# Third block's tables in a four-layer decoder trunk: VectorE makes six of eight chunks one step later, GpSimd makes the other two

## The reference, cut to what matters

```python
h = rms_norm(x, norm_mix[i]); x = x + mixer(h)
h = rms_norm(x, norm_ffn[i]); x = x + (swiglu if i % 2 == 0 else moe_swiglu)(h)
# the S5 mixer of layer 1 (64 groups of 16 channels, 64 complex states each)
mag, ang = exp(lam_re * dt), lam_im * dt;  a = mag * (cos(ang) + 1j * sin(ang))
x_t = a * x_(t-1) + B u_t;   y_t = Re(C x_t) + d * u_t;   out = GLU(gelu(y))
```

## Time and profile before

| | before |
|---|---|
| median of 3 runs | 1737.85 us |
| the profiled execution | 1736.63 us, its span 1735.1 us |
| busy, share of the span: PE, weight loads of PE | 96%, 89% |
| DVE, ACT, POOL | 75%, 58%, 12% |
| chain that ended last: PE, DVE, ACT | 75%, 10%, 6% |

### The profile page before, as it was taken

How to read it: one execution, slowest core, us unless ns; L and a number is a source line. 1 busy time by engine, 2 the same in 40 slices (tenths; PEclk the granted TensorE clock), 3 DMA queues, 4 the chain that set the end, 5 groups by cost and what they waited for, 6 DMA issues and landing times.

```text
span 1735.1 us, 26693 instructions
## 1 busy us (share of the span) xinstructions
PE 1662.9 (96%) x10979; PEld 1542.7 (89%) x10979; DVE 1295.1 (75%) x1283; ACT 1002.0 (58%) x920; POOL 214.6 (12%) x230
## 2 busy tenths in 40 slices
PE   6998999989999999999989999999999999999996
PEld 6998899878899999999879999998998999999995
DVE  5478998785688888888867555446548888888886
ACT  5554333243677777777645353335556777777773
POOL 4406991010000000000310000000000000000001
PEclk9999999989999999999999999999999999999998
DMA  7336987575489999999943254454344999999993
GB/s 305 126 119 205 309 279 263 201 277 185 146 333 365 347 373 354 380 353 357 375 145 110 75 216 182 147 192 149 120 146 183 363 352 353 375 346 368 357 382 144
DMA packets 53482, 449.28 MB, mean 259 GB/s; under 512 B 6736, under 2 KB 8944, under 8 KB 16640
## 3 DMA queue, kind: packets, MB, share of 16 engines
q1 hardware_dynamic: 48480, 430.40, 66.0%
q0 software_dynamic: 4896, 17.35, 2.8%
HBM read 426.63 MB, written 21.10 MB: 258 GB/s over the span
## 4 chain that ended last, share of the span: by engine, by line
PE 75%; DVE 10%; ACT 6%; issue 4%; DMA 3%; POOL 1%; POOLq 0%; DVEq 0%; ACTq 0%; SPq 0%
PE PS L323 22%; PE PS L325 22%; PE PS L324 22%; DVE wlo L375 3%; ACT whi L368 3%; DMA yg<-expert_rows,offi 1%; DMA expert_rows<-ysb 1%; PE PS L2119 1%; PE PS L1757 1%; PE PS L2082 1%; PE PS L2083 1%; ACT h L503 1%; PE PS L1325 1%; PE PS L916 1%; PE PS L496 1%
## 5 line engine op out<-in xcount | busy, mean ns | idle before, releaser
L375 DVE TENSOR_TENSOR wlo<-raw,whi 128x3072 fp32r<-128x3072 f32 (+1 forms) x278 | 856.3, 3082 | 181.8 <-ACT whi L368 181.0
L368 ACT ACTIVATE whi<-raw 128x3072 fp32r<-128x3072 f32 (+1 forms) x278 | 705.8, 2540 | 326.5 <-PE PS L325 310.1
L323 PE MATMUL PS<-wlo,hT_hi 128*128 128x384 f32 (+3 forms) x1840 | 594.7, 323 | 1.9 <-DVE wlo L375 1.4
L324 PE MATMUL PS<-whi,hT_lo 128*128 128x384 f32 (+3 forms) x1840 | 591.6, 322 | 0.0
L325 PE MATMUL PS<-whi,hT_hi 128*128 128x384 f32 (+3 forms) x1840 | 591.4, 321 | 0.0
L323 PEld LDWEIGHTS PS<-wlo,hT_hi 128*128 128x128 f32 x1840 | 347.7, 189 | 6.0 <-DVE wlo L375 1.7
L324 PEld LDWEIGHTS PS<-whi,hT_lo 128*128 128x128 f32 x1840 | 347.7, 189 | 2.9
L325 PEld LDWEIGHTS PS<-whi,hT_hi 128*128 128x128 f32 x1840 | 347.5, 189 | 0.3
L323 PE MATMUL PS<-wlo,mhi 128*128 128x512 f32 x352 | 143.5, 408 | 0.0
L324 PE MATMUL PS<-whi,mlo 128*128 128x512 f32 x352 | 139.1, 395 | 0.0
L325 PE MATMUL PS<-whi,mhi 128*128 128x512 f32 x352 | 139.0, 395 | 0.0
(11 more groups left out here) (392 smaller groups left out, 2073.0 us busy)
## 6 DMA issues: line engine op xcount, KB each, us to landing
raw<-in_weights SPq DMA_DIRECT2D x203, 1536.0 KB, 8.0
raw<-in_weights SPq DMA_DIRECT2D x73, 1024.0 KB, 7.1
raw<-s_tables SPq DMA_DIRECT2D x8, 1536.0 KB, 7.1
expert_rows<-ysb POOLq DMA_DIRECT2D x14, 512.0 KB, 9.7
s_tables<-g_out SPq DMA_DIRECT2D x8, 640.0 KB, 4.3
t_af<-s_rows_af SPq DMA_DIRECT2D x32, 128.0 KB, 4.0
s_tables<-g_out SPq DMA_DIRECT2D x8, 512.0 KB, 4.6
raw<-in_weights SPq DMA_DIRECT2D x3, 1152.0 KB, 9.5
```

The lines of the kernel that those rows point to most:

```text
L323: pe.matmul(o, sh, mlw, start=start, stop=False, skip_group_check=True)
L324: pe.matmul(o, sl, mh, start=False, stop=False, skip_group_check=True)
L368: act.activation(whi[p0 % SPL][:, 0:n], raw[p0 % RAW][:, 0:n], ACT.Copy).then_inc(hi_done, 1)
L375: dve.tensor_tensor(wlo[p0 % SPL][:, 0:n], raw[p0 % RAW][:, 0:n], whi[p0 % SPL][:, 0:n].bitcast(F32), ALU.subtract).then_inc(lo_done, 1)
```

## The change

Four things change. `s5_turns_dve` parts 0 to 6 move to earlier places in the attention, and only part 7 is left ahead of `proj_dve`. DVE makes the powers and taps of chunks 0 to 5 only, one dense step later than before (powers of chunk j - 1 in step j, taps of chunk j - 2 at its start), so none in step 0 and none after the last step. POOL makes those of chunks 6 and 7 in a new function, after its own eight chunks and ahead of `decay`, with loads and stores of its own queue; ACT, DVE and SP wait for these stores instead. And the four matmuls of the row of scales go behind the first `k_block`, in both attentions.

```diff
@@ sp_program
-                for c in range(KC):
-                    if p0 == base["dense0"] + ND["g", c] + SPL + RAW:
+                for c in range(DVE_TABLES):
+                    if p0 == base["dense0"] + ND["g", c + 1] + SPL + RAW:
...
-            s5_taps_store(sp, KC - 1)
@@ sb_pe
-            for b in range(3):
-                k_block(b)
+            k_block(0)
+            row_of_rs(pe, norm)
+            k_block(1)
+            k_block(2)
@@ sb_dve (a == 0): after k_out(5) parts 0 and 1, after low(4) part 2, after q_out(7) part 3,
@@ after k_out(6) part 4, after out_low(5) part 5, after softplus(7) part 6, after out_low(7) part 7
-                for part in range(4, 8):
-                    s5_turns_dve(dve, part)
+                s5_turns_dve(dve, 7)
@@ dense_dve
+        DVE_TABLES = KC - 2
-                if f == 0 and j == 0:
-                    s5_powers_dve(dve, 0)
                 if f == 0 and j >= 2:
-                    s5_taps_dve(dve, j - 1)
+                    s5_taps_dve(dve, j - 2)
...
-                if f == 0:
-                    (s5_powers_dve if j else s5_taps_dve)(dve, j)
+                if f == 0 and 1 <= j <= DVE_TABLES:
+                    s5_powers_dve(dve, j - 1)
...
-            if f == 0:
-                s5_taps_dve(dve, JD - 1)
@@ s5_tables_pool
             for b in range(2):
                 pool.wait_ge(s5_tw[b], 16 * (KC // 2))
+            s5_last_tables_pool(pool)
+        def s5_last_tables_pool(pool):
...
+            for n, c in enumerate(range(DVE_TABLES, KC)):
+                written = 16 * (KC // 2) + 32 * n
+                pool.dma_start(ff["t_bs"][:, 0, :], s5_bc[c, :, 256:512]).then_inc(s5_bs[0], 16)
+                pool.dma_start(ff["t_bs"][:, 1, :], s5_bc[c, :, 0:256]).then_inc(s5_bs[0], 16)
+                for r in range(4):
...
+                    pool.dma_start(af[32 * r:32 * r + 32].rearrange("p n q s -> p (n q s)"),
+                                   src.to_broadcast([32, 8 * P])).then_inc(s5_bs[0], 16)
+                pool.wait_ge(s5_bs[0], 16 * (KC // 2) + 96 * (n + 1))
...
+                pool.tensor_copy(o_g[:, :, :, 0, :], cn_)
+                pool.tensor_tensor(o_g[:, :, 0, 1:5, :], cr, pr, ALU.mult)
...
+                pool.dma_start(tabs[c, :, T_G], flat[:, T_G]).then_inc(s5_tw[0], 16)
+                pool.wait_ge(s5_tw[0], written + 16)
...
+                pool.tensor_tensor(o_w[:, :, 0], af[:, :, 0], b0, ALU.mult)
...
+                pool.dma_start(tabs[c, :, T_W], flat[:, 0:1024]).then_inc(s5_tw[0], 16)
+            pool.wait_ge(s5_tw[0], written + 32)
@@ s5_act, s5_dve (and s5_loads for c >= DVE_TABLES)
-            act.wait_ge(s5_gw, 16 * KC)
-            act.wait_ge(s5_ww, 16 * KC)
+            act.wait_ge(s5_gw, 16 * DVE_TABLES)
+            act.wait_ge(s5_ww, 16 * DVE_TABLES)
+            act.wait_ge(s5_tw[0], 16 * (KC // 2) + 32 * (KC - DVE_TABLES))
```

More of the change, by code:

```diff
@@ L257, in hybrid_trunk @@
                    ("ta_c", [P, ST, 8], F32), ("ta_s", [P, ST, 8], F32),
-                   ("tb_c", [P, ST, 8], F32), ("tb_s", [P, ST, 8], F32), ("t_pow", [P, ST, 2, 4], F32))
+                   ("tb_c", [P, ST, 8], F32), ("tb_s", [P, ST, 8], F32), ("t_pow", [P, ST, 2, 4], F32),
+                   ("t_af2", [P, 4, 2, P], F32))
         setup = stage(("pad_setup", [P, 42 * KB], F32),
@@ L415, in sp_program @@
                     s5_taps_load(sp, 0)
-                for c in range(KC):
-                    if p0 == base["dense0"] + ND["g", c] + SPL + RAW:
+                for c in range(DVE_TABLES):
+                    if p0 == base["dense0"] + ND["g", c + 1] + SPL + RAW:
                         s5_powers_store(sp, c)
-                        if c + 1 < KC:
+                        if c + 1 < DVE_TABLES:
                             s5_powers_load(sp, c + 1)
-                    if p0 == base["dense0"] + ND["u", c] + SPL + RAW:
+                    if p0 == base["dense0"] + ND["u", c + 1] + SPL + RAW:
                         s5_taps_store(sp, c)
-                        s5_taps_load(sp, c + 1)
-            s5_taps_store(sp, KC - 1)
+                        if c + 1 < DVE_TABLES:
+                            s5_taps_load(sp, c + 1)
             s5_loads(sp)
@@ L813, in first_columns, with row_of_rs @@
             last.then_inc(w_used, 1)
+        def row_of_rs(pe, norm):
             if norm == 0:
@@ L1210, in sb_dve @@
             k_out(5)
+            if a == 0:
+                s5_turns_dve(dve, 0)
+                s5_turns_dve(dve, 1)
             softplus(3)
@@ L1218, in sb_dve @@
             low(4)
+            if a == 0:
+                s5_turns_dve(dve, 2)
             out_low(3)
@@ L1222, in sb_dve @@
             if a == 0:
-                s5_turns_dve(dve, 0)
+                s5_turns_dve(dve, 3)
             softplus(5)
@@ L1229, in sb_dve @@
             if a == 0:
-                s5_turns_dve(dve, 1)
+                s5_turns_dve(dve, 4)
             split_lo(dve, b0 + 9)
@@ L1236, in sb_dve @@
             if a == 0:
-                s5_turns_dve(dve, 2)
+                s5_turns_dve(dve, 5)
             softplus(6)
@@ L1242, in sb_dve @@
             if a == 0:
-                s5_turns_dve(dve, 3)
+                s5_turns_dve(dve, 6)
             low(7)
@@ L1674, in s5_tables_pool @@
                 s5_decay_pool(pool, c).then_inc(s5_dec, 1)
+        def s5_last_tables_pool(pool):
+            flat = ff["t_out"][:].rearrange("p a n -> p (a n)")
+            o_g = flat[:, T_G].rearrange("p (r q i o) -> p r q i o", r=4, q=2, i=5)
+            o_w = flat[:, 0:1024].rearrange("p (n q s) -> p n q s", n=4, q=2)
+            cn_ = ff["t_bs"][:, 0, :].rearrange("p (r q o) -> p r q o", r=4, q=2)
+            bt = ff["t_bs"][:, 1, :].rearrange("p (q a s) -> p q a s", q=2, a=1)
+            pa, af = ff["t_pow"], ff["t_af2"]
+            tp = ff["t_tmp"][:].rearrange("p (r i o) -> p r i o", r=4, i=4)
+            tw = ff["t_tmp"][:].rearrange("p (n s) -> p n s", n=4)
+            for n, c in enumerate(range(DVE_TABLES, KC)):
[3 more added lines that the diff above has]
+                for r in range(4):
+                    src = afd[4 * c + r:4 * c + r + 1].rearrange("a q s -> a (q s)")
+                    pool.dma_start(af[32 * r:32 * r + 32].rearrange("p n q s -> p (n q s)"),
+                                   src.to_broadcast([32, 8 * P])).then_inc(s5_bs[0], 16)
+                pool.wait_ge(s5_bs[0], 16 * (KC // 2) + 96 * (n + 1))
+                if n >= 1:
+                    pool.wait_ge(s5_tw[0], written)
+                shape = [P, 4, 4, 32]
+                cr, ci = (cn_[:, :, q, :].rearrange("p r (a o) -> p r a o", a=1).to_broadcast(shape) for q in range(2))
+                pr, pi = (pa[:, 4 * c:4 * c + 4, q, :].rearrange("p r (i a) -> p r i a", a=1).to_broadcast(shape)
+                          for q in range(2))
+                pool.tensor_copy(o_g[:, :, :, 0, :], cn_)
+                pool.tensor_tensor(o_g[:, :, 0, 1:5, :], cr, pr, ALU.mult)
+                glink(pool, pool.tensor_tensor(tp, ci, pi, ALU.mult))
+                pool.tensor_tensor(o_g[:, :, 1, 1:5, :], cr, pi, ALU.mult)
+                glink(pool, pool.tensor_tensor(o_g[:, :, 0, 1:5, :], o_g[:, :, 0, 1:5, :], tp, ALU.subtract))
+                glink(pool, pool.tensor_tensor(tp, ci, pr, ALU.mult))
+                glink(pool, pool.tensor_tensor(o_g[:, :, 1, 1:5, :], o_g[:, :, 1, 1:5, :], tp, ALU.add))
+                pool.dma_start(tabs[c, :, T_G], flat[:, T_G]).then_inc(s5_tw[0], 16)
+                pool.wait_ge(s5_tw[0], written + 16)
+                b0, b1 = (bt[:, q].to_broadcast([P, 4, P]) for q in range(2))
+                pool.tensor_tensor(o_w[:, :, 0], af[:, :, 0], b0, ALU.mult)
+                glink(pool, pool.tensor_tensor(tw, af[:, :, 1], b1, ALU.mult))
+                pool.tensor_tensor(o_w[:, :, 1], af[:, :, 1], b0, ALU.mult)
+                glink(pool, pool.tensor_tensor(o_w[:, :, 0], o_w[:, :, 0], tw, ALU.add))
+                glink(pool, pool.tensor_tensor(tw, af[:, :, 0], b1, ALU.mult))
+                glink(pool, pool.tensor_tensor(o_w[:, :, 1], o_w[:, :, 1], tw, ALU.subtract))
+                pool.dma_start(tabs[c, :, T_W], flat[:, 0:1024]).then_inc(s5_tw[0], 16)
+            pool.wait_ge(s5_tw[0], written + 32)
@@ L1888, in s5_dve @@
             k3 = lambda a: a.rearrange("p (r k) -> p r k", r=4)
-            dve.wait_ge(s5_gw, 16 * KC)
-            dve.wait_ge(s5_ww, 16 * KC)
+            dve.wait_ge(s5_gw, 16 * DVE_TABLES)
+            dve.wait_ge(s5_ww, 16 * DVE_TABLES)
+            dve.wait_ge(s5_tw[0], 16 * (KC // 2) + 32 * (KC - DVE_TABLES))
             for c in range(KC):
@@ L1987, in s5_loads @@
                 sp.wait_ge(s5_tw[c % 2], 16 * (c // 2 + 1))
-                sp.wait_ge(s5_gw, 16 * (c + 1))
-                sp.wait_ge(s5_ww, 16 * (c + 1))
+                if c < DVE_TABLES:
+                    sp.wait_ge(s5_gw, 16 * (c + 1))
+                    sp.wait_ge(s5_ww, 16 * (c + 1))
```

(2 more changed lines are left out.)

## The result

The changed kernel takes 1744.27 us, the median of 8 runs (1742.23 to 1747.77), the kernel before 1737.82 (8 runs). The ratio is 1.0036, with a 95% interval of 1.0021 to 1.0051: slower by 0.36%, where I had forecast 1730.0 and faster. The profiled execution of the changed kernel took 1745.93 us, its span is 1744.3.

What follows compares the result with a forecast made beforehand. PE was taken as the bound, waiting in three places on DVE's table work. Of 15.2 us gained, POOL's lateness left 8.3; less 0.5 for the row gave 7.8, so 1730.0 us, range 1722 to 1738.

Steps and rivals of the forecast that it cites:

- the sum for POOL's new block: POOL ahead of norm 2: issues, landings, products, clearing and decay take 80.6 us from 260.0, reaching norm 2 at 340.6.
- 4.0 + 7.0 + 4.2 = 15.2: Us gained up to norm 2's inputs: attention's end 4.0, step 0 of the dense stage 7.0, dense end 4.2.
- The first term: Attention's end: PE's 2.71 us wait for DVE's sums and its slow clock go, 4.0 us gained.
- the third rival: Dense stage: POOL's products hold DVE, 4.6 us left over as PE's wait in steps 5 to 7; 1727.8, chance 0.10.
- the signs that I named: Trace signs: PE's two waits gone, clock 1.00, dense end 11 us earlier, POOL's power without idle, L818 behind the wait.
- The start of the block: POOL's new block begins when the eight old chunks have landed, taken 6 us earlier than before, at 260.0.
- Landings: POOL's new block: five waits, loads twice and stores three times, 5.5 us each with 0.6 counted elsewhere, 24.5 in all.
- 10.6 + 42 + 3.5 = 56.1: POOL's new block besides landings: issues 10.6 us, 24 products and two copies 42, clearing and decay 3.5.
- my first rival: POOL is in time at norm 2: landings of 3.5 us, ready at 330.6, the kernel at 1723.2; chance 0.20.
- The second rival: POOL so late the kernel is slower: landings 7.0, product factor 1.8, block 98.6 us, norm 2 at 358.6, 1748; chance 0.10.
- the point of decision: POOL's block of 89 us (348.94 - 260.0), beyond which each further us is a us lost.
- The row of scales: Second attention: its four matmuls, moved behind the first block, stand on PE's path, 0.5 us lost, between 0 and 0.6.

Runs made afterwards that it cites:

- the block left out: The changed kernel without the loads and products of POOL's two chunks, only the four stores issued: 1724.4 us, ratio 0.9918 to the kernel before.
- the parts alone: The kernel before with only the eight angle parts moved into the attention's idle stretches, tables and row of scales unchanged: 1736.9 us, ratio 0.9987.
- The run without DVE's tables: The changed kernel with DVE's table arithmetic of chunks 0 to 5 in the dense stage replaced by memsets: 1727.1 us, one run.
- the loads ahead of their use: The changed kernel with POOL's loads for its two new chunks issued earlier, the second's into its own buffer, all work done: 1729.7 us, ratio 0.9957.
- the second loads from SP: The changed kernel with the six loads for POOL's second new chunk issued from SP's queue: 1745.4 us, ratio 1.0049 to the kernel before.

## Why the prediction was wrong, point by point

Two terms of the sum for POOL's new block failed: its start (260.0, measured 269.67) and the landings of its two groups of loads (9.8 us of wait, measured 19.6). With both, POOL came to norm 2 at 356.3 instead of 340.6, 7.4 us behind the old 348.94 and not 8.3 ahead of it.

**PE's side: right without the block, 3 us short beside it.** From PE's 0.4 us wait in the attention (121.88 before) to norm 2's power the kernel before took 348.94 - 121.88 = 227.1 us; with the block left out it is 334.20 - 123.26 = 210.9. That is 16.1 less, where 4.0 + 7.0 + 4.2 = 15.2 were summed up. Counted from the start of the span it is 14.7, since the attention up to that wait took 1.4 longer in that profile. The first term shows in the parts alone, 3.8 at step 0.

In the changed kernel itself the mean is ready at 337.2, 3.0 later than with the block left out, because POOL's products hold DVE (the third rival). So two of the signs that I named came out otherwise: PE ends the dense stage 8.6 us earlier (334.71), not 11, and the mean is ready 19 us before POOL's power, not about 5. The others are there: both waits gone, clock 1.00, no idle time ahead of the power, L818's products behind the wait.

**The start of the block: wrong by 9.7 us.** I took 260.0, 6 us ahead of the old landing; it was 269.67, 3.7 behind it. Three parts make that up. Chunk 1 began 2.7 us earlier, not 4. The old store and the start behind it took 6.2 us from issue to issue, not 3.7. And the seven chunks took 15.91 us each instead of 15.35, 3.9 longer in all, where my 6 us had them 2 shorter. I had argued that POOL's delay is DVE's splits, and that these come earlier. They did come earlier, but without PE's wait and the tables of step 0 they also follow each other more closely there (the first four start within 20.8 us, 26.7 before): 14 of DVE's splits fall into the time of the seven chunks, 12 before, and as many of POOL's products are held over 2.2 us (48.8 us in all, 40.1 before). The run without DVE's tables shows the same pace-setter: eleven splits, eleven held products. So the step that failed first is that the old chunks would end earlier with the dense stage: they took longer.

**Landings: wrong by 6.0 us, in the loads.** Five waits of 4.9 beside issues were allowed, 24.5; they took 30.5. The three stores together came out below that (5.4, 3.1 and 2.4, where 14.7 stood), the two groups of loads far above (10.4 and 9.2, where 9.8 stood). My medians came from single transfers of 128 and 384 KB; a group of six, 768 KB beside 1.5 MB pieces, is not one transfer. With the loads ahead of their use the same block hides all but 0.7 us of the loads. That this kernel's 1729.7 meets the forecast's 1730.0 is luck: its block gets to work at 268.56, 8.6 us behind my 260.0, and what sets its time is DVE's mean (POOL waits 0.90 us for it), not POOL. So the sum's error was the price of two waits and a start; the other terms of the block, 10.6 + 42 + 3.5 = 56.1, measured 56.2. The start alone would have turned the sign (269.7 + 80.6 = 350.3, past 348.94); the longer block from my start would have left 2.3 us of gain (260.0 + 86.65 = 346.7).

The Trainium skill (DMA: Bandwidth & Descriptors, Anatomy of one DMA) gave an estimate of 3.5 us a landing in my first rival. The trace does not agree for the loads (8.9 and 6.3 us for 128 KB on POOL's queue) and does for the second chunk's store of 640 KB, the size for which the estimate was made (3.6 from issue to landing). The page's figure is for one DMA, and the loads shared the engines with weights at a DMA share of 0.90 (260 to 280 us).

**Products: right.** 42 us were allowed, 43.7 measured with the copies. 1.12 us alone stands against 1.04 to 1.26; beside DVE's tables one took 1.38 to 1.74, behind a split 3.3 to 4.5. The factor of 1.5 was a choice between 1 and 2.2; that it came out at 1.56 is in part luck.

**The second rival is what happened, for half of its reason.** Its end is there (norm 2 at 358.6 foretold, 356.3 measured; 1748 against 1744.3). Its factor of 1.8 on the products is not; its slow landings are, in the loads, and the late start it did not name. I gave it 0.10 because I took the start of 260.0 for certain: the range had no bound for it. By the rows I had, an old pace that does not follow the dense stage would have put the start at 266 - 4 = 262 at best, and the point of decision at a block of 87 us, not 89.

**The third rival: near in size, but not a rival.** 4.6 us were foretold for DVE's hold, 3.7 measured with the loads ahead of their use. The parts are less near: 20.6 us of hold were foretold, some 15 measured. Its sign, a wait of PE in steps 5 to 7, is in the changed kernel too (1.48 us at 317.22). It adds to whatever POOL does; with POOL in time it is what is left. The Trainium skill (SBUF — State Buffer, Who interferes with whom) says that a DVE instruction with two SBUF inputs and a GpSimd one that reads SBUF contend; the trace agrees, on both sides (1.22 instead of 0.72 us on DVE, 1.38 to 1.74 instead of 1.04 to 1.26 on POOL).

**The row of scales: right for the second attention.** 0.5 foretold, 0.46 in the trace. For the first the sum had nothing, and what the runs show there stays open.

## What to carry to other kernels

Work that is moved onto an idle engine ends when its chain of loads, products and stores ends. Price its start from what paces the work ahead of it, and give a group of loads the landing that such a group has beside the weights; then issue those loads while the work before still runs, which here turned a loss of 6 us into a gain of 8 with the same arithmetic. And an operation that the critical path needs from that engine's queue, small as it is, belongs on the list of what the move can delay.

## What the runs showed of the hardware that I had not expected

A 128x512 product of fp32 on GpSimd took 1.04 us, or 1.26 with other operands, while DVE was idle. Beside DVE's table products both engines slowed: GpSimd's to 1.38 to 1.74 us, DVE's from 0.72 to 1.22 on the mean. Behind a DVE split GpSimd's took 3.3 to 4.5 in the changed kernel.

The landing of a 128 KB load of the same tensor's rows ranged from 2.7 us (SP, ahead of the next weights) over 3.2 (SP, issued 3 us ahead of POOL's) to 8.9 (POOL's). Issued in the same 3 us, it was 7.0 on SP's queue and 6.8 on POOL's. A 640 KB store of POOL landed in 3.6 us in the changed kernel, in 7.7 with the second loads from SP and in 9.7 without VectorE's table arithmetic, the last two beside 1536 KB loads.
